# The up product of the first feed-forward block, done in seven block products for each pair of tiles

## The chip, the cores and the metric

One core of one Trainium2 chip runs the whole computation in one launch. The metric is the device time of that launch in microseconds, from the first to the last instruction and what lies around them. TensorE (PE) multiplies, VectorE (DVE), ScalarE (ACT) and GpSimd (POOL) do the rest, and SyncE (SP) issues most DMAs.

## The reference

Two transformer blocks on 1024 tokens of width 1024, all in float32. The first block is a token mixer (pooling and sparse attention) and a feed-forward block; the second is a mixer of neighbourhood attention and gated linear attention, and a feed-forward block with squared ReLU. Only the first block's feed-forward part matters here:

```python
def conv_ffn(h, w_up, conv_w, conv_b, w_down):      # D_FF = 2752, so w_up is 1024 x 5504
    u = h @ w_up
    up = jnp.pad(u, ((0, 0), (CONV_WIDTH - 1, 0), (0, 0)))
    c = conv_b + conv_w[0] * up[:, 0:S]
    for tap in range(1, CONV_WIDTH):                 # CONV_WIDTH = 3, along the tokens
        c = c + conv_w[tap] * up[:, tap:tap + S]
    gate, val = jnp.split(c, 2, axis=-1)
    return (jax.nn.silu(gate) * val) @ w_down
x = x + token_mixer(rms_norm(x, attn_norm_w), ...)
x = x + conv_ffn(rms_norm(x, ffn_norm_w), w_up, conv_w, conv_b, w_down)
```

## The kernel before

Activations lie transposed in SBUF: 128 features on the partitions, 1024 tokens along the row, eight such rows (`X`) for the width of 1024. Every large product is made of units: one unit is 128 output features for all 1024 tokens, from eight weight blocks of 128 by 128. To keep float32's accuracy each factor is split into a rounded part and a remainder (`WHI`, `WLO` for weights, `X_HI`, `HLO` for activations) and three products are added: hi by hi, hi by lo, lo by hi. So a full unit is 8 blocks x 3 products x 2 halves of 512 tokens = 48 matmuls of 128x128 by 512 columns (L248). ScalarE makes `WHI` (L215), VectorE makes `WLO` (L220), SyncE loads the raw weights two units ahead. `job_done` counts finished units, `evacuated` those whose accumulator (`PAIR`, two of them) has been read.

**The first feed-forward block** has 22 tiles of hidden features, 21 of them with a gate unit and a value unit, and one tail of 64 features whose gate and value rows share one unit: 43 up units. For each tile VectorE takes the accumulator times the norm's factor (`dve_scaled`, L371) into `UP`, ScalarE makes the affine part of the convolution (L1352), VectorE adds the two other taps (L1382, L1385), ScalarE applies SiLU (L1355), VectorE multiplies gate and value (L1390), and the product is split into `HID_HI` (L1372) and `HID_LO` (L1412), which stay in SBUF. After each eight tiles come eight down units that add into `X` (L1469), and after the last six tiles eight units of six blocks (36 matmuls). The two first units of the up product, and the two first of the last down group, are interleaved block by block (`pe_first_units`, L272). These stages are loops on every engine.

**The second feed-forward block** (from `U_WOUT`) already has its up product in another form, `pe_seven`, L2645. There weights and activations are cut into 2 by 2 blocks: a pair of units (1024 by 256 weights) by all tokens is one 2x2 block product, and it is formed from seven products of blocks instead of eight (Winograd's form; `FACTORS`). Each of the seven is 4 blocks x 3 products = 12 matmuls of 512 columns. What it needs around it:

- sums of the activations' blocks, `XSR`, split into `XSH` and `XSL`, made once while the units before it run (`pool_xs`, `dve_xs`, `act_xs_hi`, `dve_xs_lo`);
- for each pair four sums of weight blocks on GpSimd (`pool_ws`, L2274 to L2285), each waiting until the sum before in that buffer has been split;
- for each product a split of its 128x512 weight factor, three products ahead (`act_pw_hi` L2346, `dve_pw_lo` L2350);
- for each pair three copies of partial results out of PSUM on ScalarE (`act_part`, L2358), each of which TensorE waits for before a later product adds into the same bank (product 2 waits for copy 0, product 3 for copy 1, product 4 for copy 2), and on VectorE the sums that give the four output blocks (`dve_sum12` L2365, `dve_sum22` L2371, `dve_sum11` L2375 and L2379, `dve_sum21` L2384 and L2386). Product 6 waits for `dve_sum22`.

The order on each engine is written out by hand, product by product ("slot" j of pair q): first the sums or copies that product j-1 allows, then the split for product j+3. The finished rows go to DRAM (`hidden`) and come back through `HRAW` for the down units; the first eight come back in the last pair's slots (`HID_FIRST`).

Of the kernel before, what the change touches and what calls it, by code (L numbers as in the profile page):

```python
# [14 lines left out]
F32 = mybir.dt.float32  # L15
# [4 lines left out]
P = 128  # L20
T = 1024
# [76 lines left out]
def build(nc, a, out):  # L98
# [157 lines left out]
    def pe_first_units(pe, u, n):  # L256
# [48 lines left out]
    def pe_unit(pe, u, hi, lo, ready=None, outs=1, early=None):  # L305

        pe.wait_ge(w_lo, u + 1)
        for o in range(outs):
# [54 lines left out]
    def dve_weighted_lo(dve, n, k, x_k):  # L363
        dve.wait_ge(hhi_done, 8 * n + k + 1)
# [955 lines left out]
    def at_unit(u, more=0):  # L1320


        assert u >= U_G1
        return u % 2, 16 * (u // 2 + 1) + 8 * more, jobs_before(u) + more

    def act_split_at(act, u, more):
        slot, loaded, jobs = at_unit(u, more)
        if u < UNITS:
            split_hi(act, slot, loaded, jobs - 1)

    def dve_split_at(dve, u, more):
        if u < UNITS:
            split_lo(dve, u % 2, u + 1 + more)

    def pe_unit_at(pe, u, more, hi, lo, kcs=KC, ready=None):
        j = jobs_before(u)
        pe.wait_ge(w_lo, u + 1 + more)
        pe.wait_ge(evacuated, j - 1 + more)
        product(pe, u % 2, j % 2, hi, lo, kcs, 0, ready)

    def tap_of(q, b):
        return CONV[:, bass.ds(2 * q + b, 1), :].rearrange("p o c -> p (o c)")

    def act_ff1_conv(act, u, more, q):

        for b in range(2):
            act_split_at(act, u + b + 2, more)
            act.wait_ge(evacuated, jobs_before(u + b) + 1 + more)
            if b == 0:
                act.wait_ge(gv_done, q + 1)  # L1350
            tap = tap_of(q, b)
            nc.scalar.activation((CG, CV)[b][:, :], UP[:, :], ACT.Identity,  # L1352
                                 scale=tap[:, 2:3], bias=tap[:, 3:4]).then_inc(aff_done, 1)
        act.wait_ge(conv_done, 2 * q + 1)
        nc.scalar.activation(CG[:, :], CG[:, :], ACT.Silu).then_inc(silu_done, 1)  # L1355

    def act_ff1_tail(act, q):

        act_split(act, U_FF1_TAIL + 2)
        act.wait_ge(evacuated, jobs_before(U_FF1_TAIL) + 1)  # L1360
        act.wait_ge(gv_done, q + 1)
        tap = CONV[:, 2 * q, :]
        act.wait_ge(hm_ready, 2)
        nc.scalar.activation(CG[:, :], UP[:, :], ACT.Identity, scale=tap[:, 2:3], bias=tap[:, 3:4]).then_inc(aff_done, 1)
        act.wait_ge(conv_done, 2 * q + 1)
        nc.scalar.copy(CV[0:64, :], CG[64:P, :])
        nc.scalar.activation(CG[0:64, :], CG[0:64, :], ACT.Silu).then_inc(silu_done, 1)

    def act_ff1_store(act, q, p):

        act.wait_ge(gv_done, q + 2)
        nc.scalar.copy(HID_HI[:, bass.ds(p, 1), :], GV[:, :].unsqueeze(1)).then_inc(hid_hi, 1)  # L1372

    def dve_ff1_conv(dve, u, more, q):
        for b in range(2):
            dve_split_at(dve, u + b + 2, more)
            c, tap = (CG, CV)[b], tap_of(q, b)
            if b or u > U_FF1:
                dve.wait_ge(conv_done, 2 * q + b)
            dve_scaled(dve, 1, jobs_before(u + b), UP, more)  # L1380
            dve.wait_ge(aff_done, 2 * q + b + 1)
            nc.vector.scalar_tensor_tensor(c[:, 1:T], UP[:, 0:T - 1], tap[:, 1:2], c[:, 1:T],  # L1382
                                           ALU.mult, ALU.add).then_inc(tap_done, 1)
            dve.wait_ge(tap_done, 2 * q + b + 1)
            nc.vector.scalar_tensor_tensor(c[:, 2:T], UP[:, 0:T - 2], tap[:, 0:1], c[:, 2:T],  # L1385
                                           ALU.mult, ALU.add).then_inc(conv_done, 1)
        dve.wait_ge(silu_done, q + 1)
        dve.wait_ge(conv_done, 2 * q + 2)
        dve.wait_ge(hid_lo, q + 1)
        nc.vector.tensor_tensor(GV[:, :], CG[:, :], CV[:, :], ALU.mult).then_inc(gv_done, 1)  # L1390

    def dve_ff1_tail(dve, q):

        dve_split(dve, U_FF1_TAIL + 2)
        tap = CONV[:, 2 * q, :]
        dve.wait_ge(hm_ready, 2)
        dve.wait_ge(conv_done, 2 * q)
        dve_scaled(dve, 1, jobs_before(U_FF1_TAIL), UP)
        dve.wait_ge(aff_done, 2 * q + 1)
        nc.vector.scalar_tensor_tensor(CG[:, 1:T], UP[:, 0:T - 1], tap[:, 1:2], CG[:, 1:T],  # L1400
                                       ALU.mult, ALU.add).then_inc(tap_done, 1)
        dve.wait_ge(tap_done, 2 * q + 1)
# [7 lines left out]
    def dve_ff1_store(dve, q, p):  # L1410
        dve.wait_ge(hid_hi, q + 1)
        nc.vector.tensor_tensor(HID_LO[:, bass.ds(p, 1), :], GV[:, :].unsqueeze(1),  # L1412
                                HID_HI[:, bass.ds(p, 1), :].bitcast(F32), ALU.subtract).then_inc(hid_lo, 1)

    def pe_ff1(pe):
        hi, lo = (lambda k: HID_HI[:, k, :]), (lambda k: HID_LO[:, k, :])
        pe_first_units(pe, U_FF1, 1)
        with pe.Fori(0, FF1_FULL) as g:
            with pe.Fori(0, GROUP) as p:
                for b in range(2):  # L1420
                    pe_unit_at(pe, U_FF1 + 2 + b, 24 * g + 2 * p, hi_of(1), h_lo)
            with pe.Fori(0, KC // 2) as t:
                pe.wait_ge(hid_lo, GROUP * g + GROUP + 1)
                for b in range(2):
                    pe_unit_at(pe, U_FF1 + 2 + 2 * GROUP + b, 24 * g + 2 * t, hi, lo)
        with pe.Fori(0, FF1_REST - 2) as p:
            for b in range(2):
                pe_unit_at(pe, U_FF1_REST + b, 2 * p, hi_of(1), h_lo)
        pe_unit_at(pe, U_FF1_TAIL, 0, hi_of(1), h_lo)
        tile_ready = lambda k: pe.wait_ge(hid_lo, GROUP * FF1_FULL + k + 2)  # L1430
        for part in range(2):
            for b in range(2):
                u = U_Z2 - KC + b
                j = jobs_before(u)
                if not part:
                    pe.wait_ge(w_lo, u + 1)
                    pe.wait_ge(evacuated, j - 1)
                product(pe, u % 2, j % 2, hi, lo, FF1_REST - 1 + part, 0, None if b else tile_ready,
                        part * (FF1_REST - 1), part == 1)
        with pe.Fori(1, KC // 2) as t:  # L1440
# [1597 lines left out]
```

## Time and profile before

| | us |
|---|---|
| median of 3 runs | 3111.73 |
| lowest, highest | 3110.82, 3114.38 |
| the profiled execution's own time | 3114.16 |
| its span, first to last instruction | 3112.1 |
| TensorE busy in it | 3030.7 |
| VectorE busy | 1580.9 |
| ScalarE busy | 1266.6 |
| GpSimd busy | 489.9 |

The profile is of one execution. Its own time is 2.1 us more than its span, and 2.4 us above the median of the runs. Matmuls are pipelined: a matmul's row lasts longer than the step to the next one, so the step between starts is what counts, not the length. A few records of matmuls are missing from the trace.

### The profile page before, as it was taken

To read this page: it belongs to the slowest core of one execution; us is meant where nothing else is said; L and a number is where in the kernel's file an instruction comes from. 1 tells how busy PE (TensorE), PEld (TensorE's weight loads), DVE (VectorE), ACT (ScalarE), POOL (GpSimd) and SP (SyncE) were. 2 spreads that over 40 slices of the span, in tenths; PEclk is the share of its full clock that TensorE was granted. 3 is DMA by queue.
4 is the path that set the end of the run, shared out by engine and by line. 5 is a ranking of instruction groups with operands and counts; after the bars stand their busy time and mean duration, and the time that the engine had idled before them with its cause. 6 is when DMAs were issued, how large, how long until landed. Compare 5 with 4: busy or idle time off the path is not lost.

```text
span 3112.1 us, 42590 instructions
## 1 busy us (share of the span) xinstructions
PE 3030.7 (97%) x16760; PEld 2490.6 (80%) x16760; DVE 1580.9 (51%) x2426; ACT 1266.6 (41%) x1999; POOL 489.9 (16%) x688
## 2 busy tenths in 40 slices
PE   8999998899999999999999999999999999999998
PEld 6888887789988878888888888656878788878887
DVE  6653257667763445534542552465654755543334
ACT  4652137877773233212221341365643543431122
POOL 0110007755542000000000000120012322200000
PEclk9999998999999999999999999999999999999999
DMA  4222320000004311111111131100102233242322
GB/s 144 82 75 75 114 88 15 2 2 2 1 2 151 99 42 54 47 47 47 47 47 52 49 123 58 34 1 21 41 28 75 102 110 117 99 162 95 95 75 75
DMA packets 61189, 201.96 MB, mean 65 GB/s; under 512 B 9840, under 2 KB 13040, under 8 KB 60640
## 3 DMA queue, kind: packets, MB, share of 16 engines
q1 hardware_dynamic: 50048, 159.52, 15.6%
q0 software_dynamic: 10976, 40.15, 3.6%
q8 instruction: 114, 1.87, 0.3%
q14 instruction: 51, 0.42, 0.0%
HBM read 160.32 MB, written 33.55 MB: 62 GB/s over the span
## 4 chain that ended last, share of the span: by engine, by line
PE 91%; ACT 4%; DVE 3%; issue 2%; DMA 0%; POOL 0%; SPq 0%; DVEq 0%; ACTq 0%; POOLq 0%
PE PS L248 60%; PE PS L2645 9%; PE PS L902 3%; PE PS L916 3%; PE PS L888 2%; PE PS L887 2%; PE PS L1692 2%; PE PS L272 1%; PE PS L1719 1%; PE PS L1704 1%; ACT P_SHORT L986 1%; PE PS L939 1%; PE PS L2671 1%; ACT PT L996 1%; PE PS L930 1%
## 5 line engine op out<-in xcount | busy, mean ns | idle before, releaser
L215 ACT CAST WHI<-RAW 128x1024 fp32r<-128x1024 f32 x185 | 194.5, 1052 | 1118.7 <-PE PS L248 1094.7
L220 DVE TENSOR_TENSOR WLO<-RAW,WHI 128x1024 fp32r<-128x1024 f32 x185 | 226.7, 1225 | 606.3 <-ACT WHI L215 604.0
L248 PE MATMUL PS<-HLO,WHI 128*128 128x512 f32 x1648 | 508.1, 390 | 0.0
L248 PEld LDWEIGHTS PS<-HLO,WHI 128*128 128x128 f32 x1648 | 309.7, 188 | 64.9
L248 PE MATMUL PS<-X_HI,WHI 128*128 128x512 f32 x1008 | 312.9, 392 | 2.2 <-DVE W L371 2.2
L248 PE MATMUL PS<-X_HI,WLO 128*128 128x512 f32 x1008 | 310.9, 390 | 0.0
L248 PE MATMUL PS<-HID_HI,WHI 128*128 128x512 f32 x832 | 256.3, 389 | 2.5 <-DVE W L2375 1.3
L248 PE MATMUL PS<-HID_LO,WHI 128*128 128x512 f32 x832 | 256.2, 389 | 0.0
L248 PE MATMUL PS<-HID_HI,WLO 128*128 128x512 f32 x832 | 256.2, 389 | 0.0
L248 PEld LDWEIGHTS PS<-X_HI,WHI 128*128 128x128 f32 x1008 | 188.5, 188 | 44.5 <-DVE W L371 2.7
L248 PEld LDWEIGHTS PS<-X_HI,WLO 128*128 128x128 f32 x1008 | 189.5, 188 | 39.6
L248 PEld LDWEIGHTS PS<-HID_HI,WHI 128*128 128x128 f32 x832 | 156.0, 188 | 35.6 <-DVE W L2375 1.7
L248 PEld LDWEIGHTS PS<-HID_HI,WLO 128*128 128x128 f32 x832 | 156.2, 188 | 32.5
L248 PEld LDWEIGHTS PS<-HID_LO,WHI 128*128 128x128 f32 x832 | 156.2, 188 | 32.4
L248 PE MATMUL PS<-HHI,WHI 128*128 128x512 f32 x512 | 160.1, 394 | 2.7 <-DVE WLO L220 2.7
L248 PE MATMUL PS<-HHI,WLO 128*128 128x512 f32 x512 | 157.6, 389 | 0.0
L1469 DVE TENSOR_TENSOR XB<-XB,PS 128x1024 f32<-128x1024 f32 x30 | 36.6, 1221 | 217.4 <-PE PS L248 217.4
L887 PE MATMUL PS<-KHD,QS 128*128 128x512 f32 (+3 forms) x384 | 136.7, 363 | 4.9 <-DVE HMIN L1075 2.6
L1097 POOL TENSOR_SCALAR P_LONG<-P_LONG,HINV,GATE 128x640 f32<-128x640 f32 (+3 forms) x128 | 121.0, 956 | 93.7 <-DVE HINV L1080 93.3
L986 ACT ACTIVATE P_LONG<-P_LONG,HMIN 128x640 f32<-128x640 f32 (+3 forms) x128 | 116.7, 914 | 38.2 <-DVE HMIN L1075 37.5
L1528 POOL DMA_DIRECT2D x_kept<-X x8 | 4.2, 534 | 793.9 <-DVE X L1307 793.9
L996 ACT COPY PT<-PS 128x512 f32<-128x512 f32 x216 | 116.6, 590 | 20.9 <-PE PS L902 19.4
(401 smaller groups left out, 5910.6 us busy)
## 6 DMA issues: line engine op xcount, KB each, us to landing
RAW<-in_w SPq DMA_DIRECT2D x187, 512.0 KB, 3.5
W<-in_w SPq DMA_DIRECT2D x16, 1024.0 KB, 4.9
hidden<-W SPq DMA_DIRECT2D x32, 512.0 KB, 2.6
W<-hidden SPq DMA_DIRECT2D x32, 512.0 KB, 4.6
X<-in_x SPq DMA_DIRECT2D x8, 512.0 KB, 7.9
Q<-QN POOLq DMA_DIRECT2D x32, 128.0 KB, 2.7
merged<-W POOLq DMA_DIRECT2D x8, 512.0 KB, 3.3
W<-gate POOLq DMA_DIRECT2D x8, 512.0 KB, 4.0
```

Source lines behind the costliest of these rows:

```text
L215: nc.scalar.copy(WHI[:, slot, :], RAW[:, slot, :]).then_inc(w_hi, 1)
L220: nc.vector.tensor_tensor(WLO[:, slot, :], RAW[:, slot, :], WHI[:, slot, :].bitcast(F32), ALU.subtract).then_inc(w_lo, 1)
L248: last = nc.tensor.matmul(o[:, half], w[:, slot, cols], x(k)[:, half], start=(k == 0 and w is WHI and x is hi), stop=(done and k == kcs - ...
L887: nc.tensor.matmul(out, QS[s % 2][:, j, :], KHD[g][:, branch, c:end], start=True, stop=False)
L888: last = nc.tensor.matmul(out, QS[s % 2][:, j, :], KLD[g][:, branch, c:end], start=False, stop=True)
L902: last = nc.tensor.transpose(turn_ps(c)[:, P * (2 * x + e):P * (2 * x + e) + P], src, IDENT[:, :])
L916: last = nc.tensor.matmul(out_ps(m)[half_of(e), :], (VS, VW)[branch][:, kt, g], PT[u % 8][:, 2 * x + e, :], start=False, stop=(u + 1 == us ...
L986: nc.scalar.activation(p, p, ACT.Exp, scale=-1.0, bias=HMIN[:, n % 8, branch:branch + 1], accum_out=HSUM[:, n % 8, branch:branch + 1]).the ...
L996: nc.scalar.copy(PT[u % 8][:, 0:n, :], turn_ps(c)[:, 0:P * n].rearrange("p (x q) -> p x q", q=P))\
L1097: nc.gpsimd.tensor_scalar(p, p, HINV[:, n % 8, branch:branch + 1], GATE[:, qt, col:col + 1], ALU.mult, ALU.mult).then_inc(p_done, 1)
L1692: nc.tensor.matmul(NS_PS[n % 4], QST[n % 4][:, :], KA[:, hp, 64 * start:64 * start + 512], start=True, stop=True).then_inc(ns_done, 1)
L2645: last = nc.tensor.matmul(out2, wt[n % 4][:, cols], xt[x][:, k, :], start=(i in (0, 1, 5) and k == 0 and xt is XSH and wt is PWH), stop=(k ...
```

## The change

The first feed-forward block's up product takes the form that the second block's has. `Seven` is a class that holds what both uses need (`S1`, `S2`), and the functions get it as an argument. In `S1` an item is one tile: its gate unit and its value unit are the pair. There are 21 pairs of seven products, and the tail of 64 + 64 rows is an item of four products of its own (`TAIL_FACTORS`), put last but one. All products come first; every tile's gated rows go to DRAM (`hidden1`), and the down product follows in three groups of 8, 8 and 6 tiles, its tiles read back. The eight units before (`U_WO`) take over the making of the activations' sums. The loops of the stage are gone. The weights' order in DRAM follows. The second block's code is the same work with other names.

```diff
+    class Seven:
...
+    S1 = Seven("1", None, 1, X, U_WO, U_FF1, ["pair"] * (FF1_TILES - 2) + ["tail", "pair"],
...
+    HID1_FIRST = {1: (0,), 2: (1,), 4: (2,), 5: (3, 4), 6: (5,)}
...
+    TAIL_FACTORS = (("A11", "B11", "z"), ("A11", "T1", "w"), ("A12", "B22", "w"), ("A12", "B21", "z"))
...
+    def act_ff1_slot(act, q, i):
...
+        if i == 0:
+            act_affine(act, q, 1)
+        if i == 1:
+            act_silu(act, q)
+
+    def dve_ff1_slot(dve, q, i):
...
+        elif i == 0:
+            dve_tap1(dve, q, 0)
+            dve_tap0(dve, q, 0)
+        elif i == 1:
+            dve_tap1(dve, q, 1)
+        elif i == 2:
+            dve_tap0(dve, q, 1)
+        if i == 3:
+            dve_gated(dve, q)
...
+    def act_seven1(act):
+        for j, (q, i) in enumerate(S1.products):
+            act_seven_slot(act, S1, j)
+            act_ff1_slot(act, q - 1, i)
+            if i == 6:
+                act_affine(act, q, 0)
+            if q == Q_LAST1:
+                for h in HID1_FIRST.get(i, ()):
+                    act_hid1_hi(act, h)
+                if i == 5:
+                    act_first_down(act, S1, 0)
...
+    def dve_seven1(dve):
+        for j, (q, i) in enumerate(S1.products):
+            dve_seven_slot(dve, S1, j)
+            dve_ff1_slot(dve, q - 1, i)
+            if q == Q_LAST1:
+                for h in HID1_FIRST.get(i, ()):
+                    dve_hid1_lo(dve, h)
+                if i == 5:
+                    dve_split(dve, U_FF1)
+
+    def dve_ff1_down(dve):
+        dve_sum21(dve, S1, Q_LAST1)
+        dve_ff1_slot(dve, Q_LAST1, 0)
+        for h in (6, 7):
+            dve_hid1_lo(dve, h)
+        dve_split(dve, U_FF1 + 1)
+        for i in range(1, 4):
+            dve_ff1_slot(dve, Q_LAST1, i)
+        for d in range((FF1_GROUPS - 1) * KC):
+            dve_add_residual(dve, U_FF1 + d, 0, X, d % KC)
+            dve_split(dve, U_FF1 + d + 2)
+            if GROUP + d < FF1_TILES:
+                dve_hid1_lo(dve, GROUP + d)
+        dve_residual(dve, U_Z2 - KC, 2, X, lambda t: X[:, t, :], lambda t: None)
...
+    def sp_hidden1(sp, h):
+
+        g, k = divmod(h, GROUP)
+        q = TILE_OF.index(h)
+        sp.wait_ge(hid_out[0], 16 * (q + 1))
+        if h >= 4:
+            sp.wait_ge(hid_lo, h - 3)
+        if g == 0:
+            if k == 4:
+                sp.wait_ge(up_done, S1.up0[Q_LAST1] + 1)
+            elif k == 5:
+                sp.wait_ge(pw_lo, S1.prods)
+            else:
+                sp.wait_ge(prod_done, S1.done(Q_LAST1, (0, 0, 3, 3, None, None, 5, 5)[k]))
+        elif g == 1:
+            sp.wait_ge(prod_done, S1.prods)
+        else:
+            sp.wait_ge(job_done, jobs_before(U_FF1 + KC * (g - 1)))
+        sp.dma_start(HID1_RAW[g % 2][k][:, :], hidden1[h]).then_inc(HID1_IN[h % 4], 16)
...
+        for h in range(GROUP):
+            if h == 2:
+                store(Q_LAST1 - 1)
+            sp_hidden1(sp, h)
...
+    def pe_ff1_down(pe):
+        for d in range(FF1_GROUPS * KC):
+            g = d // KC
+            if d < 2:
+                pe.wait_ge(up_done, S1.up0[Q_LAST1] + (3, 5)[d])
+            ready = None if d % KC else lambda k: pe.wait_ge(hid_lo, GROUP * g + k + 1)
+            pe_unit(pe, U_FF1 + d, lambda k: HID1_HI[g % 2][k][:, :], lambda k: HID1_LO[g % 2][k][:, :], ready=ready,
+                    kcs=FF1_REST if g == FF1_GROUPS - 1 else KC)
...
     def pool_second(pool):
 
-        pool.wait_ge(merged_done, KC)
+        pool.wait_ge(prod_done, S1.prods)
...
-        pe_ff1(pe)
+        pe_seven(pe, S1)
+        pe_ff1_down(pe)
```

`act_affine` is the affine part of the convolution (gate b=0, value b=1), `dve_tap1` and `dve_tap0` the two taps, `act_silu` and `dve_gated` as before, each of tile q-1 in the slots of item q. `dve_sum11` and `dve_sum21` multiply by the norm's factor where the second block also takes the ReLU.

## Rows read from the trace of the kernel before

**Rows 1.** The page: busy time, share of span and instructions of TensorE.

```profile
PE 3030.7 (97%) x16760; PEld 2490.6 (80%) x16760; DVE 1580.9 (51%) x2426; ACT 1266.6 (41%) x1999; POOL 489.9 (16%) x688
```

**Rows 2.** Chain of waits, 1040 to 1900: start us, length us, what.

```profile
1135.03 10.89 PE PS L272 x48
...
1159.57 1.15 DVE W L371
...
1160.76 637.00 PE PS L248 x2802
...
1799.01 1.15 DVE WLO L220
...
1849.53 10.89 PE PS L272 x48
```

**Rows 3.** TensorE's timeline in the first up product: first and last of 49 rows.

```profile
1299.83 0.62 PE L248 MATMUL PS<-X_HI,WHI 128*128 128x512 f32 x2
...
1321.59 0.62 PE L248 MATMUL PS<-X_HI,WHI 128*128 128x512 f32 x2
```

**Rows 4.** Chain of waits, 2330 to the end.

```profile
2432.04 5.44 PE PS L2645 x24
2437.48 4.53 issue
2442.01 8.38 PE PS L2645 x24
2450.39 1.72 PE PS L325 x4
2452.11 277.46 PE PS L2645 x1224
...
2749.13 326.69 PE PS L248 x1440
```

**Rows 5.** VectorE by line and form, 2460 to 2740 (seven products): count | busy us, mean ns.

```profile
L2350 DVE TENSOR_TENSOR PWL<-WS_S,PWH 128x512 fp32r<-128x512 f32 x59 | 40.5, 687 | 23.5 <-ACT PWH L2346 23.2
...
L2379 DVE SCALAR_TENSOR_TENSOR W<-W,W 128x1024 f32<-128x1024 f32 x15 | 18.9, 1261 | 0.5
L2386 DVE SCALAR_TENSOR_TENSOR W<-W,W 128x512 f32<-128x512 f32 x15 | 17.0, 1131 | 0.0
...
L2375 DVE TENSOR_TENSOR W<-PART,PS 128x512 f32<-128x512 f32 x14 | 9.6, 688 | 18.5 <-PE PS L2645 18.5
```

**Rows 6.** VectorE by line and form, 1140 to 1790 (first feed-forward block).

```profile
L1382 DVE SCALAR_TENSOR_TENSOR W<-W,CONV,W 128x1023 f32<-128x1023 f32 x42 | 53.9, 1284 | 72.2 <-ACT W L1352 72.2
...
L1390 DVE TENSOR_TENSOR W<-W,W 128x1024 f32<-128x1024 f32 x21 | 25.7, 1225 | 1.9
```

**Rows 7.** ScalarE by line and form, 2460 to 2740.

```profile
L2346 ACT CAST PWH<-WS_S 128x512 fp32r<-128x512 f32 x58 | 35.8, 617 | 58.8 <-PE PS L2645 58.8
...
L2358 ACT COPY PART<-PS 128x512 f32<-128x512 f32 x45 | 26.1, 581 | 44.8 <-PE PS L2645 44.8
```

**Rows 8.** ScalarE by line and form, 1140 to 1790.

```profile
L1352 ACT ACTIVATE W<-W,CONV 128x1024 f32<-128x1024 f32 x42 | 52.2, 1244 | 115.7 <-DVE W L371 115.7
L1355 ACT ACTIVATE W<-W 128x1024 f32<-128x1024 f32 x21 | 21.9, 1045 | 0.0
```

**Rows 9.** GpSimd's timeline: start us, length us, what, idle before.

```profile
2422.69 1.74 POOL L2278 TENSOR_TENSOR WS_S<-WS_S,W 128x512 f32<-128x512 f32 x1
...
2555.42 1.29 POOL L2278 TENSOR_TENSOR WS_S<-WS_S,W 128x512 f32<-128x512 f32 x1 [2.52 <-DVE PWL L2350]
```

**Rows 10.** VectorE's timeline at the same times.

```profile
2423.31 1.67 DVE L2260 SCALAR_TENSOR_TENSOR XSR_T<-XB,NORM_W,XSR_T 128x512 f32<-128x512 f32 x1
...
2556.12 1.14 DVE L2386 SCALAR_TENSOR_TENSOR W<-W,W 128x512 f32<-128x512 f32 x1
```

**Rows 11.** ScalarE's timeline, last pair of the second block's up product.

```profile
2736.26 1.05 ACT L2407 CAST HID_HI<-W 128x1024 fp32r<-128x1024 f32 x1 [2.67 <-DMA W<-hidden]
```

**Rows 12.** The page: DMA issues, KB each, median us from issue to landing.

```profile
W<-hidden SPq DMA_DIRECT2D x32, 512.0 KB, 4.6
```

More of the change, by code:

```diff
@@ L1344, in act_ff1_conv @@
[L1344 to L1355, printed above, removed]
@@ L1369, in act_ff1_store @@
[L1369 to L1390, printed above, removed]
@@ L1410, in dve_ff1_store @@
[L1410 to L1440, printed above, removed]
-            for b in range(2):
-                pe_unit_at(pe, U_Z2 - KC + b, 2 * t, hi, lo, FF1_REST)
@@ L2288, in pool_seven, with pool_seven1, pool_seven2 @@
+    def pool_seven1(pool):
+        for t in range(4):
+            pool_xs(pool, S1, t)
+        for q, kind in enumerate(S1.items):
+            if kind == "pair":
+                pool_ws(pool, S1, q)
+    def pool_seven2(pool):
         pool.wait_ge(gl_lo, GLA_HEADS)
@@ new lines, in act_part, with dve_sum12, dve_sum22 @@
+        nc.scalar.copy(c.part[i][:, :], c.banks[q % 2]["zwz"[i]]).then_inc(part_done, 1)
+    def dve_sum12(dve, c, q):
+        dve.wait_ge(prod_done, c.done(q, 3))
+        dve.wait_ge(part_done, c.part0[q] + 3)
+        if c is S2 and q:
+            dve.wait_ge(hid_out[0], 16 * (FF1_TILES + q))
+        nc.vector.tensor_tensor(c.up[0][:, HI_COLS], c.part[2][:, :], c.banks[q % 2]["w"], ALU.add).then_inc(up_done, 1)
+    def dve_sum22(dve, c, q):
+        dve.wait_ge(prod_done, c.done(q, 4))
+        if c is S2 and q:
+            dve.wait_ge(hid_out[1], 16 * q)
+        nc.vector.tensor_tensor(c.up[1][:, HI_COLS], c.part[1][:, :], c.banks[q % 2]["z"], ALU.add).then_inc(up_done, 1)
@@ new lines, in build, with convs_before, act_affine @@
+    Q_TAIL = S1.items.index("tail")
+    def convs_before(q, b=0):
+        return 2 * q + b - (1 if q > Q_TAIL else 0)
+    def act_affine(act, q, b):
+        n_up = 4 if b == 0 and q != Q_TAIL else 6 if b else 3
+        act.wait_ge(up_done, S1.up0[q] + n_up)
+        if b:
+            if q:
+                act.wait_ge(hid_out[0], 16 * q)
+        elif q:
+            act.wait_ge(gv_done, q)
+        if q == Q_TAIL:
+            act.wait_ge(hm_ready, 2)
+        tap = CONV[:, 2 * TILE_OF[q] + b, :]
+        nc.scalar.activation((CG, CV)[b][:, :], S1.up[b][:, :], ACT.Identity,
+                             scale=tap[:, 2:3], bias=tap[:, 3:4]).then_inc(aff_done, 1)
@@ new lines, in act_seven_slot @@
+    def act_seven_slot(act, c, j):
+        q, i = c.products[j]
+        if i in (1, 2, 3) if c.items[q] == "pair" else i == 1:
+            act_part(act, c, q, i - 1)
+        if j + 3 < len(c.products):
+            act_pw_hi(act, c, j + 3)
+        if q == 0 and i < 4:
+            for m, k in XS_AFTER[i]:
+                act_xs_hi(act, c, m, k)
+        if j == 4:
+            act_rstd(act, c.norm)
+    def act_seven1(act):
[3 more added lines that the diff above has]
+            if i == 6:
+                act_affine(act, q, 0)
+            if q == Q_LAST1:
[3 more added lines that the diff above has]
+                    act_first_down(act, S1, 0)
@@ L2557, in dve_wout, with dve_seven_slot @@
                 for m, k in XS_TURN:
-                    dve_xs_lo(dve, m, k)
-    def dve_seven(dve):
-        for j in range(PRODS + 1):
-            q, i = divmod(j, NP)
+                    dve_xs_lo(dve, c, m, k)
+    def dve_seven_slot(dve, c, j):
+        q, i = c.products[j]
+        if c.items[q] == "pair":
             if i == 4:
-                dve_sum12(dve, q)
+                dve_sum12(dve, c, q)
             if i == 5:
-                dve_sum22(dve, q)
+                dve_sum22(dve, c, q)
@@ new lines, in dve_seven_slot @@
+        if i == 0 and q:
+            if c.items[q - 1] == "pair":
+                dve_sum21(dve, c, q - 1)
+            else:
+                dve_tail_lo(dve, q - 1)
+        if j + 3 < len(c.products):
+            dve_pw_lo(dve, c, j + 3)
+        if j == 0:
+            dve_acc(dve, c.norm, KC - 1)
+        if q == 0 and i < 4:
+            for m, k in XS_AFTER[i]:
+                dve_xs_lo(dve, c, m, k)
+    def dve_seven1(dve):
[7 more added lines that the diff above has]
+                    dve_split(dve, U_FF1)
@@ L2580, in dve_seven, with dve_seven2 @@
+    def dve_seven2(dve):
+        for j, (q, i) in enumerate(S2.products):
+            dve_seven_slot(dve, S2, j)
+            if q == Q_LAST2:
+                for h in HID_FIRST.get(i, ()):
                     dve_hid_lo(dve, h)
@@ L2582, in dve_seven @@
                     dve_split(dve, U_FF2)
+        dve_sum21(dve, S2, Q_LAST2)
     def dve_ff2_down(dve):
```

744 lines of the change are left out of this document (393 added, 351 removed).

## The prediction

> **What bounds the kernel now.** I read the page first: TensorE is busy for 97% of the span [rows 1]. A busy share alone can hide a slow step, so next I read how far apart its matmuls start. In the first block's up product 49 rows of two matmuls go from 1299.83 to 1321.59 [rows 3]: 21.76 us / 96 = 0.2267 us for each. Then the chain of waits over the stage [rows 2]: from the first up matmul (1135.03) to the first of the next stage (1849.53) are 714.5 us, nearly all of it TensorE. Counted from the code the stage has 43 x 48 up and 16 x 48 + 8 x 36 down = 3120 matmuls: 707.2 us, and 1.7 for the norm's mean; 5.5 us are left, in gaps behind the interleaved units (the chain leaves TensorE at 1159.57 and 1799.01). So the stage costs what its matmuls cost, and only fewer matmuls, or new gaps, can move it.
>
> The second block shows what the new form does on this chip. From 2452.11 the chain is TensorE alone, 277.46 us for 1224 matmuls [rows 4], 0.2267 each: same step, no gap, in spite of a new weight factor for each matmul. Only its ends cost something.
>
> **What goes.** 21 gate units and 21 value units are 21 x 96 = 2016 matmuls; as pairs they are 21 x 84 = 1764. The tail is 48 either way, the down product 1056 either way. 252 matmuls go: 252 x 0.2267 = 57.1 us. The 5.5 us of old gaps go with the code that made them. So 62.6 us at most, if nothing new stands on TensorE's path.
>
> **What comes at the start.** The units before must now also make the sums of X. In the second block that work came late for product 2: 24 matmuls in 5.44 us, then nothing for 4.53, then 24 in 8.38 [rows 4]. The missing 2.94 us are matmuls whose starts lie wider apart just after the idle time. The order on every engine is copied, and X is ready as early there, so I take the same 4.53 + 2.94 = 7.5 us. Bounds: 4.5 (no slow matmuls) to 10.
>
> **What comes in each pair.** TensorE takes 84 x 0.2267 = 19.04 us for one, a product 2.72. All else must fit beside it. VectorE, from [rows 5, 6]: seven splits 7 x 0.69, the four sums that read PSUM 4 x 0.69, the value tile's second half times the norm 0.69, the gate tile times the norm 1.22 (the length of L1390's form), four taps 4 x 1.28, gate by value 1.22: 15.8 us. ScalarE [rows 7, 8]: seven splits 7 x 0.62, three copies 3 x 0.58, two affine parts 2 x 1.24, SiLU 1.05: 9.6 us. Both fit, VectorE with 3.2 us to spare.
>
> But GpSimd's four sums of weights, 1.29 us each [rows 9], disturb VectorE. The one that starts at 2555.42 ends at 2556.71, and the VectorE multiplication that starts at 2556.12 in between, both of its inputs in SBUF, lasts 1.14 instead of 0.69 [rows 9, 10]: it ends 0.55 after GpSimd does. At 2423.31 a three-operand form takes 1.67, while GpSimd's own sum beside it takes 1.74 [rows 9, 10]: they take turns. The taps and the product of gate and value read two inputs from SBUF too, and here they stand in slots 0 to 3, just where the second block left VectorE idle for GpSimd. Worst case: all four sums block, 15.8 + 4 x 1.29 = 21.0 us, 2.0 over. I laid the pair out by these lengths, zero being TensorE's start of product 0, and with engines seeing a product's end some 0.2 later. VectorE: two halves of dve_sum21 to 2.0 (one blocked for 0.5), split to 2.6, first gate tap to 3.8, GpSimd's third sum to 5.0, second gate tap to 6.1, split, first value tap to 7.9, GpSimd's fourth sum to 9.0, split, second value tap to 10.8, split, gate by value to 12.5, dve_sum12 to 13.1 (2 late), split, and at 13.8 dve_sum22 is on time again. GpSimd's first sum falls into an idle stretch. So about two and a half sums block, and the pair closes with TensorE never waiting for a sum: product 6 starts at 16.3, dve_sum22 is done at 14.5. The narrow place is on ScalarE: SiLU is queued ahead of the copy of partial 1. It waits for the second gate tap (6.1), runs to 7.1, the copy to 7.7, and TensorE wants product 3 at 8.16. 0.45 us to spare. I count nothing per pair, with bounds 0 and 2.0.
>
> The Trainium skill, page "SBUF — State Buffer", section "Who interferes with whom", says that VectorE and GpSimd share one port pair as an exclusive lock: a VectorE instruction with two SBUF inputs and a GpSimd instruction that reads SBUF block each other for the whole length of the one that came first. That speaks against this change, which puts five long instructions of that kind beside GpSimd in each pair. The trace agrees with its 1.14 and 1.67 us for half tiles. By the rule at its worst the pair is the 21.0 us of rival 2; by the layout it costs nothing, since GpSimd is held up as well and its sums are not urgent.
>
> **What comes at the end.** The first eight hidden tiles must be back from DRAM and split before the down product. The last pair's slots get eight splits of 1.22 us on VectorE and eight of 1.05 on ScalarE, in order, so they stand before copies and sums that TensorE wants. In the second block two tiles were fetched long before, and yet ScalarE waited 2.67 us for one DMA [rows 11]; from 2432.04 to the down product at 2749.13 are 317.1 us [rows 4], less 1344 x 0.2267 = 304.7, the mean's 1.7 and the start's 7.5, so that end cost 3.2 us. Here it is worse in two places. (a) Tile 0 is fetched only after product 0 of the last pair (2.7), lands 4.6 later at the median [rows 12] and is split to 8.5, before partial 1 is copied: product 3 starts 0.8 late. Behind it stand the tail's copy and SiLU and tile 1's split, so partial 2 comes at 13: product 4 is 1.2 late. (b) SP issues the fetch of tile 2 behind the tail tile's store, which waits for VectorE's gate by value: VectorE comes 3 late out of the tail (taps of tile 19 packed in four products, and four sums of GpSimd in a row), so that is at about 16. Tile 2 lands about 20.5, is split on both engines to 22.7, and dve_sum22 stands behind it, at 23.4: product 6, due at 18.4, starts 5.0 late and its twelve matmuls are wide apart, 2.6 to 2.9 more. The last splits then hold up the first down unit by some 0.4. Sum: 0.8 + 1.2 + 5.0 + 2.8 + 0.4 = 10.2 us. Bounds 3.2 (as in the second block) and 14 (twice the DMA's wait).
>
> Nothing is added later. The groups' other tiles have a down unit of 10.9 us each for one fetch, one 1.05 and one 1.22 split; the constants that pool_second loads are wanted hundreds of microseconds on.
>
> **Sum.** 2868 x 0.2267 + 1.7 + 7.5 + 10.2 = 669.6 us instead of 714.5: 44.9 less. Against the profiled execution, 3114.2 - 44.9 = 3069.3; that one lies 2.4 above the median, so the median should be 3111.7 - 44.9 = 3067.
>
> **Rivals.**
> 1. *A cheap end.* Tiles land in 3 us and the tail's VectorE lag is small: the end costs the second block's 3.2 instead of 10.2, so 3060. For it: the copy of its order. Against: tile 2's place behind the store.
> 2. *VectorE becomes the bound.* All four GpSimd sums block in every pair: 21 x 2.0 = 41 us back, 3108. For it: the port's price is in [rows 10]. Against: the first sum meets an idle or PSUM-reading VectorE.
> 3. *Product 3 waits a little in each pair.* If the second gate tap is 0.9 later than I laid it out, TensorE waits 0.45 x 20 = 9 us: 3076.
> 4. *Slower.* The same place, partial 1's copy behind SiLU, with GpSimd getting its turn before both gate taps and the split between them: two more blocks of up to 1.74 [rows 9] put the tap at 9.6, SiLU to 10.7, the copy to 11.3, 3.1 late in each of 20 pairs: 62 us, 3129. It decides from 2.2 us a pair (44.9 / 20). Against: GpSimd has only four sums, and two of them are due in slots 5 and 6.
>
> **Numbers.** Chances: the forecast 0.60 (its own range 3062 to 3073), rival 1 0.12, rival 3 0.18, rival 2 0.05, rival 4 0.05. The range runs from rival 1's side to past rival 3's: 3056 to 3084, leaving out rivals 2 and 4 and a bit of each tail. A measurement of this kernel tells about 0.2% (6 us) from no change. Faster 0.91, the same 0.03 (rival 2 in part), slower 0.06 (rival 4, and what I overlook of it).
>
> **What would show it.** From the first seven-product matmul to the next stage's first interleaved unit 670 us. The chain there is TensorE at 0.2267 a matmul from product 4 of pair 0 to the last pair. One gap of some 4.5 before product 2 of pair 0, and gaps before products 3, 4 and 6 of the last pair, the last of them released by dve_sum22. VectorE's taps last 1.28 or about 2.3 by turns. The prediction is wrong if TensorE's waits name the partial copies in every pair, or if the chain runs through VectorE's taps.

## The result, and the profile after

The changed kernel takes 3086.7 us (median of 4 runs, 3083.5 to 3091.1), the kernel before, beside it on the same chip, 3113.1. The ratio is 0.9916, with an interval of 0.9899 to 0.9934: 26.4 us faster, where 45 were forecast, and 2.7 us outside the range.

The page of the execution profiled (its own time is 3091.09 us), with the chain's shares by engine:

```profile
span 3089.3 us, 41962 instructions
...
PE 2993.6 (97%) x16508; PEld 2455.4 (79%) x16508; DVE 1743.7 (56%) x2650; ACT 1345.9 (44%) x2191; POOL 666.6 (22%) x780
...
PE 83%; DVE 9%; ACT 4%; issue 3%; DMA 1%; POOL 0%; SPq 0%; ACTq 0%; DVEq 0%; POOLq 0%
```

TensorE is still busy for 97% of the span. The share tells nothing of the loss; the chain does, which now runs through VectorE for 9%. Its pieces in the stage (start, length, what), which answer to [rows 2] and [rows 4]:

```profile
1139.65 5.44 PE PS L2786 x24
1145.09 4.58 issue
1149.67 8.15 PE PS L2786 x24
...
1294.29 8.46 PE PS L2786 x36
...
1303.49 1.22 DVE W L2273
...
1310.17 2.21 DVE W L2331
...
1314.08 8.46 PE PS L2786 x36
...
1511.98 27.50 PE PS L2786 x120
...
1557.42 6.25 DMA HID_RAW<-hidden
...
1573.53 5.13 DMA HID_RAW<-hidden
...
1595.22 231.49 PE PS L256 x1020
1826.71 10.89 PE PS L280 x48
```

The first unit of the next stage begins at 1826.71, so the stage takes 687.1 us; it took 714.5 [rows 2], and 669.6 were predicted. The group from 1294.29 to 1314.08 is one pair, and it repeats: from 1195.34 to 1511.98 are 316.64 us for 16 pairs, 19.79 each, where 84 matmuls take 19.04. So the account of the stage is

| us | predicted | measured |
|---|---|---|
| 2868 matmuls at 0.2267, and the mean | 651.9 | 651.9 |
| start (issue 4.58, and 8.15 where 24 matmuls take 5.44) | 7.5 | 7.3 |
| pairs (16 x 0.75, and 0.4 in the first one that waits) | 0 | 12.4 |
| end | 10.2 | 15.2 |
| stage | 669.6 | 686.8 |

The end is 1595.22 less 1511.98, 83.2 us, less the 22 products (59.84) up to the down product and the 36 matmuls (8.16) ahead of 1595.22. The 0.3 us that the sum lacks of 687.1 are what my counting of gaps leaves over.

The stage is 27.4 us shorter, the span only 22.8. The other 4.6 lie ahead of the change: this stage begins at 1139.65 instead of 1135.03 [rows 2]. Most of it arises in a stretch of the attention stage, which the change doesn't touch (busy time of each engine; the number after POOL's is the granted clock of TensorE), in the kernel after:

```profile
400.00:600.00 200.00, 186.75 (x1318) 160.64 (x1318) 126.76 (x416) 131.04 (x333) 95.03 (x140) 0.91 0.10 35
```

and in the kernel before:

```profile
400.00:600.00 200.00, 180.82 (x1339) 154.91 (x1338) 128.51 (x427) 134.67 (x342) 98.49 (x144) 0.96 0.10 35
```

Laid side by side, ScalarE's instructions of the two traces are 0.5 us apart at 423 us of the kernel before, 3.7 at 575 and 4.6 at 676. The clock granted there differs between executions; that it accounts for all of the 3.2 us is a reading, not a test. In the executions of the experiments the span less the stage is 2395 to 2402 us, whatever was edited: a single time can't tell 5 us, a stage's length in the trace can. It is not free of chance either: the wait at the start, 4.6 us here, is 5.5 in e1 and 3.7 in e2, and e1's edit doesn't touch it.

**Where a pair's 0.75 us go.** Instructions by time (start, length, and in brackets the idle time before it with its releaser) in the stretch that ends with a pair's product 3 at 1314.08:

```profile
1303.49 1.22 DVE L2273 TENSOR_TENSOR W<-W,W 128x1024 f32<-128x1024 f32 x1
...
1303.77 2.10 POOL L2158 TENSOR_TENSOR WS_S<-W 128x512 f32<-128x512 f32 x1 [8.24 <-DMA W<-in_w]
...
1304.63 1.79 DVE L2243 TENSOR_TENSOR PWL<-WS_S,PWH 128x512 fp32r<-128x512 f32 x1
...
1306.50 1.29 POOL L2162 TENSOR_TENSOR WS_S<-WS_S,W 128x512 f32<-128x512 f32 x1 [0.63 <-DVE PWL L2243]
...
1306.94 1.40 DVE L2283 TENSOR_TENSOR W<-W,W 128x512 f32<-128x512 f32 x1
...
1309.02 2.27 POOL L2166 TENSOR_TENSOR WS_S<-W,WS_S 128x512 f32<-128x512 f32 x1 [1.23 <-DVE PWL L2243]
...
1310.17 2.20 DVE L2331 SCALAR_TENSOR_TENSOR W<-W,CONV,W 128x1022 f32<-128x1022 f32 x1
...
1312.40 1.06 ACT L2341 ACTIVATE W<-W 128x1024 f32<-128x1024 f32 x1 [1.80 <-DVE W L2331]
1313.37 0.57 ACT L2251 COPY PART<-PS 128x512 f32<-128x512 f32 x1
...
1314.08 0.47 PE L2786 MATMUL PS<-XSH_B,PWH 128*128 128x512 f32 x1 [0.47 <-ACT PART L2251]
```

Read it from the bottom. Product 3 waits for the copy of partial 1 (L2251, 1313.37). The copy stands behind SiLU (L2341), which had to wait for the second gate tap (L2331), done at 1312.37. Between VectorE's instructions GpSimd's sums get their turns: the split at 1304.63 lasts 1.79 instead of 0.69, the half multiplication 1.40, the tap 2.20 instead of 1.28. TensorE started the pair at 1305.29: product 3 was due at 1313.45, one step behind the matmul before it (1313.22), and three products go off that. I had laid out `dve_sum21` done 2.0 after it; it is done at 1308.34, 3.05 after. The tap is 7.1 after it instead of 6.1, the copy 8.65 instead of 7.7, and 8.16 was the limit.

The first of the sums is the one out of place. It should have run while VectorE was idle, and was released by a DMA. SyncE's issues in the kernel after:

```profile
1297.91 0.37 SPq L2550 DMA_DIRECT2D W<-in_w  x1
1299.04 0.34 SPq L2555 DMA_DIRECT2D hidden<-W  x1
```

and in the second block of the kernel before, where a pair starts at 2555.31, with GpSimd's first sum:

```profile
2546.49 0.38 SPq L2486 DMA_DIRECT2D W<-in_w  x1
...
2551.61 1.29 POOL L2274 TENSOR_TENSOR WS_S<-W 128x512 f32<-128x512 f32 x1 [9.22 <-DVE PWL L2350]
...
2555.86 0.32 SPq L2491 DMA_DIRECT2D hidden<-W  x1
```

There the pair's 1 MB of weights are asked for 8.8 us ahead of the pair's start, and are no longer waited for 3.7 ahead of it, when a split releases the sum. Here they are asked for 7.4 ahead, since VectorE's last splits of the pair before come later, a store follows 1.1 us behind, and they are there 5.9 us after their issue, 1.5 ahead of the start at 1305.29. So they are issued 1.4 us later, and take longer too: 4.7 to 5.1 us for the eleven loads of the second block, 5.6 to 6.0 for the sixteen from 1198.96 to 1495.80. The stage's loads at 1139.7 and 1159.4, behind which no store is issued so soon, took 4.8 us here too. That points at the store; no run moved it. The second block is near the same edge: in its next pair, at 2570.65, the DMA is what releases the first sum. Ahead of the pair that starts at 1305.29 VectorE is idle from 1301.4 to 1302.8; its weights, there at 1303.77, miss that by a microsecond.

**Where the end's 15.2 us go.** SyncE's queue, and the two gaps of TensorE:

```profile
1555.76 0.33 SPq L2555 DMA_DIRECT2D hidden<-W  x1
1556.13 1.20 SPq L2572 DMA_DIRECT2D RAW<-in_w  x2
1557.42 0.91 SPq L2413 DMA_DIRECT2D HID_RAW<-hidden  x2
...
1565.37 0.77 PE L2786 MATMUL PS<-XSH_B,PWH 128*128 128x512 f32 x1 [4.13 <-ACT PART L2251]
...
1573.11 0.32 SPq L2555 DMA_DIRECT2D hidden<-W  x1
1573.53 2.16 SPq L2413 DMA_DIRECT2D HID_RAW<-hidden  x4
...
1581.72 0.77 PE L2786 MATMUL PS<-XSH_T,PWH 128*128 128x512 f32 x1 [5.15 <-DVE W L2264]
```

Tile 0 is fetched at 1557.42, behind a store and two loads of the down weights, and lands at 1563.69. ScalarE takes its split first and the copy of partial 1 after it, so TensorE stands idle for 4.13 us. After that its matmuls are 0.427 us apart until 1571.4; the granted clock says what that is:

```profile
1565.40:1570.60 5.20, 5.20 (x12) 4.11 (x13) 2.95 (x4) 4.38 (x6) 0.00 (x0) 0.50 0.00 0
```

0.50 is the lower level, 1.2 GHz. In gaps between starts, less one step, and in what the wide steps cost, place (a) makes 4.29 + 2.86 = 7.15 us, and place (b), at 1581.72, 5.31 + 1.61 = 6.92. One more microsecond goes before 1595.22, to the last tiles' splits.

### The profile page after: what moved, and what is told of

Read it like the earlier page. It is cut to its first block, busy times and chain, and to the rows that moved or that the text cites. A ratio compares the mean times of both kernels' runs of the same rounds, so it can differ in the third digit from the quotient of the medians.

```text
span 3089.3 us, 41962 instructions
## 1 busy us (share of the span) xinstructions
PE 2993.6 (97%) x16508; PEld 2455.4 (79%) x16508; DVE 1743.7 (56%) x2650; ACT 1345.9 (44%) x2191; POOL 666.6 (22%) x780
## 4 chain that ended last, share of the span: by engine, by line
PE 83%; DVE 9%; ACT 4%; issue 3%; DMA 1%; POOL 0%; SPq 0%; ACTq 0%; DVEq 0%; POOLq 0%
PE PS L256 46%; PE PS L2786 16%; PE PS L912 3%; PE PS L926 3%; PE PS L898 2%; PE PS L897 2%; PE PS L1531 2%; DVE PWL L2243 1%; DVE W L2331 1%; PE PS L1558 1%; PE PS L1543 1%; PE PS L949 1%; ACT P_SHORT L996 1%; DVE W L2273 1%; DVE W L2283 1%
## 5 line engine op out<-in xcount | busy, mean ns | idle before, releaser
L256 PE MATMUL PS<-HLO,WHI 128*128 128x512 f32 x992 | 306.5, 390 | 0.0
L256 PE MATMUL PS<-HID_HI,WHI 128*128 128x512 f32 x832 | 256.5, 389 | 2.4 <-DVE W L2268 1.6
L256 PE MATMUL PS<-HID_LO,WHI 128*128 128x512 f32 x832 | 256.2, 389 | 0.0
L256 PE MATMUL PS<-HID_HI,WLO 128*128 128x512 f32 x832 | 256.0, 389 | 0.0
L2786 PE MATMUL PS<-XSH_T,PWH 128*128 128x512 f32 x596 | 236.2, 396 | 15.5 <-issue 9.1
L2786 PE MATMUL PS<-XSL_T,PWH 128*128 128x512 f32 x596 | 234.5, 393 | 0.0
L2786 PE MATMUL PS<-XSH_T,PWL 128*128 128x512 f32 x596 | 234.2, 393 | 0.0
L256 PEld LDWEIGHTS PS<-HLO,WHI 128*128 128x128 f32 x992 | 186.7, 188 | 39.3
L2786 PE MATMUL PS<-XSH_B,PWH 128*128 128x512 f32 x456 | 180.1, 395 | 12.1 <-ACT PART L2251 12.1
L256 PEld LDWEIGHTS PS<-HID_HI,WHI 128*128 128x128 f32 x832 | 156.0, 188 | 35.5 <-DVE W L2268 2.0
L256 PEld LDWEIGHTS PS<-HID_LO,WHI 128*128 128x128 f32 x832 | 156.2, 188 | 32.6
L256 PEld LDWEIGHTS PS<-HID_HI,WLO 128*128 128x128 f32 x832 | 156.2, 188 | 32.3
L2786 PE MATMUL PS<-XSH_B,PWL 128*128 128x512 f32 x456 | 178.7, 392 | 0.0
L2786 PE MATMUL PS<-XSL_B,PWH 128*128 128x512 f32 x456 | 178.5, 391 | 0.0
L256 PE MATMUL PS<-HHI,WHI 128*128 128x512 f32 x512 | 160.7, 395 | 2.7 <-DVE WLO L228 2.7
L256 PE MATMUL PS<-HHI,WLO 128*128 128x512 f32 x512 | 158.1, 390 | 0.0
L2239 ACT CAST PWH<-WS_S 128x512 fp32r<-128x512 f32 x148 | 90.9, 616 | 138.7 <-PE PS L2786 138.7
L2786 PEld LDWEIGHTS PS<-XSH_T,PWH 128*128 128x128 f32 x596 | 113.4, 190 | 42.0 <-issue 17.9
```

What stands on the lines that cost most here:

```text
L256: last = nc.tensor.matmul(o[:, half], w[:, slot, cols], x(k)[:, half], start=(k == 0 and w is WHI and x is hi), stop=(done and k == kcs - ...
L2239: nc.scalar.copy(c.pwh[n % 4][:, :], c.raw_of(n)).then_inc(pw_hi, 1)
L2786: last = nc.tensor.matmul(c.banks[q % 2][b], wt[n % 4][:, cols], xt[x][:, k, :], start=(opens and k == 0 and xt is c.xsh and wt is c.pwh), ...
```

## The experiments

Before each, the theory it tests was written down. The ratios are to the kernel before, run beside each on the same chip. *A* below is the reading above: the copy behind SiLU in each pair, and the fetched tiles' splits ahead of copies and sums at the end.

| | edit | us (runs) | ratio and interval | stage |
|---|---|---|---|---|
| after | | 3086.7 (4) | 0.9916, 0.9899 to 0.9934 | 687.1 |
| e1 | SiLU one slot later | 3077.5 (4) | 0.9889, 0.9872 to 0.9905 | 675.2 |
| e2 | GpSimd's sums 64 columns | 3071.9 (1) | | 671.8 |
| e3 | value tile's weights first | 3072.4 (1) | | 672.8 |
| e4 | tiles read back later | 3080.0 (4) | 0.9901, 0.9885 to 0.9918 | 678.6 |
| e5 | e1 and e4 | 3068.3 (5) | 0.9850, 0.9837 to 0.9864 | 667.2 |
| e6 | e1, e3 and e4 | 3066.9 (1) | | 664.5 |
| e7 | e5, other order of X sums | 3070.0 (4) | 0.9858, 0.9843 to 0.9873 | 667.1 |
| e8 | after, other order of X sums | 3085.4 (1) | | 687.2 |
| e9 | e6's kernel once more | 3065.5 (5) | 0.9849, 0.9836 to 0.9862 | 664.5 |
| e10 | e9, last taps behind splits | 3067.4 (5) | 0.9850, 0.9837 to 0.9862 | 664.3 |

### e1: SiLU one slot later

```diff
-        if i == 1:
+        if i == 2:
             act_silu(act, q)
...
-        act_ff1_slot(act, Q_LAST1, 1)
+        act_ff1_slot(act, Q_LAST1, 2)
...
```

> SiLU goes from slot 1 to slot 2 on ScalarE, behind the copy of partial 1; nothing else moves. Theory A: in each pair TensorE waits 0.75 us because that copy is queued behind SiLU, and nothing else is short; so the step from pair to pair falls from 19.79 to 19.04 us, the waits for the partial copies in pairs 2 to 18 go, and the stage (first seven-product matmul to the next stage's first unit) falls from 687.1 to about 674.6. Theory B: VectorE is the bound (18.1 us busy of 19.79, and it is blocked by GpSimd); then TensorE's wait moves to another signal of VectorE and the step stays at 19.5 or more, the stage at 684 or more.

Measured: stage 675.2, 11.9 less. The chain of waits has one piece of TensorE from the first pair to the one ahead of the tail:

```profile
1158.52 367.22 PE PS L2786 x1620
```

1620 x 0.2267 is 367.2, so all 12.4 us of the pairs' waits are gone; the start is 0.6 dearer in this execution. SiLU still waits for the second gate tap, and the copy of partial 1 has gone ahead of it:

```profile
1305.44 0.59 ACT L2251 COPY PART<-PS 128x512 f32<-128x512 f32 x1 [0.32 <-PE PS L2786]
...
1306.91 1.06 ACT L2341 ACTIVATE W<-W 128x1024 f32<-128x1024 f32 x1 [0.37 <-DVE W L2331]
```

VectorE's instructions have kept their lengths, splits of 1.78 and taps of 2.20. So it isn't VectorE's load that holds TensorE up but one instruction's place in ScalarE's order.

### e2: sums of 64 columns

```diff
-        s1, s2, s4, s3 = (c.ws[m][:, :] for m in ("S1", "S2", "S4", "S3"))
+        n = 64 if c is S1 and q else 512
+        s1, s2, s4, s3 = (c.ws[m][:, 0:n] for m in ("S1", "S2", "S4", "S3"))
...
```

> GpSimd's four sums of weights cover 64 of their 512 columns from the second pair on (the other columns keep old values, so the products are of other numbers), same count and same signals. Theory A: what makes SiLU late is GpSimd's sums blocking VectorE; with sums of some 0.3 us all VectorE instructions have their plain lengths (taps 1.28, splits 0.69), the second gate tap ends 1.5 us or more earlier, the step is 19.04 us and the stage about 674.6, with SiLU where it was. Theory B2: the port has little to do with it, the gate tap is late because of VectorE's own queue; then the step stays within 0.2 of 19.79.

Measured: stage 671.8. The waits of the pairs are gone here too, with SiLU at its old place: taps last 1.28, splits 0.69. GpSimd's blocks are what made the tap late. The stage is 2.8 us shorter than expected, which I hadn't counted: 2.3 at the end, where TensorE's wait for the copy in the last pair is 2.6 instead of 4.1 us and fewer matmuls are wide apart, and 0.6 at the start.

### e3: the value tile's weights first

The pair's weights come in two DMAs of 512 KB with a semaphore each; the first sum needs the value tile's alone.

```diff
-                sp.dma_start(S1.w7[q % 2][:, :, :], a["w"][at_q:at_q + 2].rearrange("h p n -> p h n"))\
-                    .then_inc(pair_in[q % 2], 16)
+                sp.dma_start(S1.w7[q % 2][:, 1, :], a["w"][at_q + 1]).then_inc(second_in[q % 2], 16)
+                sp.dma_start(S1.w7[q % 2][:, 0, :], a["w"][at_q]).then_inc(pair_in[q % 2], 16)
...
```

> The weights of a pair come in two DMAs of 512 KB instead of one of 1 MB, the value tile's first, and GpSimd's first sum, which needs only that, waits for it alone. Theory A: the step that failed is where the first sum falls. It now starts some 2 us earlier, in the stretch in which VectorE waits for product 5, so the gate multiplication (1.22) and the split after it (0.69) are not blocked, dve_sum21 is done 1.0 us earlier, and the step is 19.04 us, the stage about 675. Rival: the four sums cost VectorE the same wherever they fall, and the step stays at 19.6 or more.

Measured: stage 672.8. The same stretch by time:

```profile
1313.33 1.29 POOL L2159 TENSOR_TENSOR WS_S<-W 128x512 f32<-128x512 f32 x1 [6.39 <-DVE PWL L2247]
...
1315.22 1.22 DVE L2277 TENSOR_TENSOR W<-W,W 128x1024 f32<-128x1024 f32 x1
1316.37 0.68 DVE L2247 TENSOR_TENSOR PWL<-WS_S,PWH 128x512 fp32r<-128x512 f32 x1
```

The first sum waits for a split, no longer for the DMA, and is over before the gate multiplication starts: 1.29 us, the split behind it 0.68. The second gate tap still lasts 2.20, and yet TensorE doesn't wait. One block too many was the whole difference. Of the 2 us under the expected stage, the end again has the most (waits of 2.9 and 5.9 us, with fewer matmuls wide apart). Three different edits (e1 to e3) each remove all of the wait.

### e4: the tiles read back later

```diff
-    HID1_FIRST = {1: (0,), 2: (1,), 4: (2,), 5: (3, 4), 6: (5,)}
+    HID1_FIRST = {3: (0,), 4: (1,), 6: (2, 3, 4, 5)}
...
-            if h == 2:
+            if h == 4:
                 store(Q_LAST1 - 1)
```

> Only the last item changes: the first hidden tiles are split in slots 3, 4 and 6 (one, one, four tiles) instead of slots 1, 2, 4, 5, 6, and SyncE issues the fetches of tiles 2 and 3 before the tail tile's store. Theory A: the end costs 15.2 us because splits that wait for DMAs stand ahead of the copy of partial 1 (4.1 us) and of dve_sum22 (5.2 us plus slow matmuls); both waits go, the down product starts within 2 us of its due time, and of 15.2 us some 4 stay (stage about 676), with a wait of 1 to 2 us for the splits of tiles 6 and 7. Rival: the DMAs themselves are late (6 us each behind one another), so the wait moves to the down unit's own blocks and no more than 5 us are won (stage 682 or more).

Measured: stage 678.6, 8.5 less; about 676 had been expected. TensorE's waits in the stage (total, times, longest):

```profile
PE PS L2786 <- ACT PART L2251: 8.7, 18, 0.6
...
PE PS L256 <- DVE HID_LO L2423: 3.2, 2, 2.5
PE PS L2786 <- DVE W L2264: 1.4, 1, 1.4
```

The waits of 4.1 and 5.2 us have fallen to 0.6 and 1.4, and the pairs' stay. What I had underrated is the wait of the down unit (L256): four tiles are now split at the very end, and the first down unit waits 0.7 us for the first of them and 2.5 for tile 6.

### e5: both

> SiLU in slot 2 and the new order at the end together. Theory A: the two losses are apart (pairs 2 to 18, and the last item), so the gains add: stage 687.1 - 11.9 - 8.5 = 666.7 us, and the whole kernel about 20 us under the changed kernel. Rival: with SiLU later, the tail's gate by value and store come later too and eat part of the end's gain; then 669 or more.

Measured: stage 667.2, against 687.1 - 11.9 - 8.5 = 666.7. The gains add up to within 0.5 us: the two losses are independent.

### e6 and e9: all three

> The same with the pair's weights in two DMAs, the value tile's first. Theory A: in the pairs either edit alone already takes the wait away, so both together give nothing more there; only VectorE's lag out of the tail can be smaller. Stage within 1.5 us of the run without it. Rival: the port's blocks cost something besides product 3; then 3 us or more less.

> The run with SiLU in slot 2, two weight DMAs and the new end once more, timed. In the profile before its stage was 664.5 us, 22.6 under the changed kernel's 687.1, and no edit touches another stage. Theory A: 3086.7 less 22.6 is about 3064 us. Rival: the 2.7 us that its stage was under the run without the two DMAs are chance (a stretch of wide-apart matmuls in the down product); then its stage comes out at 667 here.

Measured: stage 664.5 in both, 2.7 us less than e5, more than the 1.5 expected of e6. The chain of e9:

```profile
1156.67 388.98 PE PS L2791 x1716
...
1569.72 231.52 PE PS L256 x1020
```

It runs on TensorE alone for 389 us, into the last pair. From 1156.67 to the last piece's start are 413.05 us, in e5 414.10: 1.05 us come from the end, where e5 still waits 0.6 us for a copy. The other 1.6 are matmuls of e5's down product around 1571 to 1574, whose starts lie wide apart behind the wait for the last tiles (granted clock 0.79 from 1568 to 1576); e9 waits 2.5 us at the same place too and has no such stretch. Nor has e4, which waits there as long and has its weights in one DMA, so the stretch doesn't hang on that edit alone; whether the edit has a part in it is open. In time the two kernels can't be told apart: their intervals are nearly the same.

### e7 and e8: another order of the X sums

```diff
-    XS_TURN = [("B11", k) for k in range(4)] + [("B22", k) for k in range(3)] + T_OF(2)
+    XS_TURN = [("B11", k) for k in range(4)] + [("T2", 2)]
...
```

The rest of B22 and T3 is made after the last rows of X, behind T2's.

> SiLU and end as before, and a new order of the splits of the activations' sums at the start, in both blocks: before TensorE's product 0 only those that products 0 to 2 need (5 instead of 10 on VectorE), the rest behind. Theory A for the start: the gap of 4.6 us before product 2 comes from VectorE, which adds the last unit to X 5 us late behind ten splits, so ScalarE's copy of partial 0 is late; with five fewer splits (3.3 us) the gap falls to about 1.3 us and the matmuls behind it are wide apart for less long. Each block wins 3 to 6 us; stage about 662. Rival: the gap is set by GpSimd's sums beside dve_xs (blocked to 1.65 us each), and stays above 3.5 us.

> The new order at the start alone, on the changed kernel. Theory A: 3 to 6 us less in each block's first pair, the rest of the stage as it was (step 19.79 us, end 15 us): stage 681 to 684. Rival as in the run with all three: the gap stays above 3.5 us, stage 686 or more.

Measured: stages 667.1 and 687.2, nothing won: both miss. In e7 the wait before product 2 has fallen from 4.6 to 0.5 us, and come back behind it:

```profile
1141.09 0.47 PE L2787 MATMUL PS<-XSH_T,PWH 128*128 128x512 f32 x1 [0.50 <-issue]
...
1144.01 0.50 PE L2787 MATMUL PS<-XSH_T,PWH 128*128 128x512 f32 x1 [0.64 <-DVE XSL_T L2221]
...
1147.47 0.77 PE L2787 MATMUL PS<-XSH_B,PWH 128*128 128x512 f32 x1 [2.48 <-DVE XSL_B L2225]
```

Behind the last one the granted clock is 0.50 again. The second block, which has the new order too, wins 0.9 us at its start in e7 (18.8 us from its first matmul to product 4, against 19.7 in e5), not 3. The theory that the order of the X sums costs the start its time has fallen. VectorE is at work without a break from the last rows of X until product 3, and what is moved ahead of one product comes late for the next. That reading is from the traces alone; no run made that work smaller.

### e10: the last taps behind the last splits

```diff
-        dve_ff1_slot(dve, Q_LAST1, 0)
         for h in (6, 7):
             dve_hid1_lo(dve, h)
         dve_split(dve, U_FF1 + 1)
+        dve_ff1_slot(dve, Q_LAST1, 0)
```

> The same, and at the turn to the down product VectorE splits tiles 6 and 7 and the second weights before the last gate tile's two taps, not behind them. Theory A: TensorE waited 0.7 and 2.5 us for splits of hidden tiles in the first down unit, the second time behind 2.6 us of taps; that wait falls to 1 us or less, the stage by about 1.5 to 2.5 us. Rival: tile 7's DMA lands too late for it (ScalarE waited 0.7 us for it), and less than 1 us is won.

Measured: stage 664.3, 0.2 less. The first down unit still waits 3.0 us, 2.3 of them for tile 6. The chain ahead of it:

```profile
1559.92 4.63 DVE HID_LO L2427 x4
...
1565.79 1.24 ACT W L2323
1567.04 0.94 ACT HID_HI L2422
...
1568.00 1.24 DVE HID_LO L2427
...
1569.28 231.53 PE PS L256 x1020
```

So under 1 us is won, as the rival said, but not for its reason. ScalarE waited 0.2 us for tile 7's DMA, behind this; tile 6 was fetched at 1561.2 and landed 4.3 us later, 1.4 before ScalarE split it. What stood ahead of the split was the value tile's affine part (L2323, 1565.79), which waits for `dve_sum21` behind VectorE's four splits. Again it is an order on ScalarE; no run changed it.

## Why the prediction came out as it did

**What was right.** The step of 0.2267 us and the 252 matmuls that go: 2868 of them and the mean fill the stage but for the named losses. The start, taken from the second block's own start at 7.5 us, is 7.3. The place of every wait that came is in the text: product 3 behind the copy behind SiLU, the copies and `dve_sum22` of the last pair behind tiles 0 and 2. Rival 1 is out, the end cost 15.2. Rival 2 is out: VectorE is busy for 18.1 of 19.8 us in a pair, not the bound, as e1 shows by leaving its load alone. Rival 4 too; the tap was 1.0 late, not 3.5.

**What failed** is the term per pair, taken as 0 for "GpSimd's first sum falls into an idle stretch". It doesn't, since it waits for its weights. I had copied the second block's idle stretch without asking when the DMA in front of it is issued and what is issued beside it: 1.4 us later than there, with a store at its heels and a landing some 0.8 us longer, so that the sum starts 2.2 us later. With all four sums blocking instead of two and a half, VectorE was about 1 us late, and the margin was 0.45. TensorE's waits name the partial copies in the pairs from 2 to 18, the sign by which the prediction called itself wrong. Rival 3 named this place with 9 us for a tap 0.9 later. It was 12.4, since TensorE's restart costs more than the copy's delay: the copy ended 0.49 behind the limit, product 3 was due at 1313.45 and came at 1314.08, 0.63 late, the step behind its first matmul is 0.30, and all in all a pair loses 0.75. e1 took these waits away.

In the new rows a sum of GpSimd behind a running multiplication of VectorE takes 2.10 us, and the split behind that sum 1.79. The Trainium skill, page "SBUF — State Buffer", section "Who interferes with whom", has it that a VectorE instruction with two SBUF inputs contends with a GpSimd instruction that reads SBUF, and that the order of issue decides which of them waits; the rows agree. The error was not in the rule but in when the sum started.

**What was mis-sized** is the end, 15.2 instead of 10.2. Place (b) was worked out at 5.0 + 2.8 and measured 5.3 + 1.6. Place (a) was put at 0.8 + 1.2 and measured 7.15: I took the fetch of tile 0 as issued at once and 4.6 us long, without the store and the two weight loads that stand ahead of it on SyncE (issued at 1555.76 to 1557.3), and it took 6.25. And I gave wide-apart matmuls to the longer wait only, though a wait of 4.1 us has them too. The last tiles were 0.4 and measured 1.0.

**The rest.** The 4.6 us ahead of the stage are of the profiled execution: the medians differ by 26.4 us, the stages of the two profiles by 27.4, so that of the two spans' 22.8 the missing part is nearly all chance.

The best version, e9, has the repairs of e1, e3 and e4: 3065.5 us. That it comes so near the 3067 forecast for a kernel without a wait in its pairs is in part luck: its end costs some 5 us where 10.2 were forecast, and its stage is 5.1 us under the 669.6. The start still costs 7.

## What to carry to other kernels

When a schedule is copied from another stage, look at when its DMAs are issued and not only at its engines' order: a buffer freed one or two microseconds later shifts the one instruction that everything was laid around. Where a layout leaves TensorE less than a microsecond, take the wait as the likely case, and look, in the queue of the engine that TensorE waits for, for the instruction that nobody wants soon (here SiLU on ScalarE, 11.9 us for one line moved). At the turn between two stages, list all that stands in a DMA queue ahead of the first fetch, and put the splits of what is fetched behind the copies that TensorE waits for.

## What the runs showed of the hardware

- After idle times of 4.1, 4.6 and 5.2 us TensorE's matmuls are 0.427 us apart instead of 0.227, at a granted clock of 0.50, and that costs 1.6 to 2.9 us more. After the 0.47 us in each pair they aren't. After 2.6 us in e2's last pair they are too, at 1.7 us more. After 2.5 us in the first down unit they were in e5 and e7, and not in e4, e6 and e9.
- GpSimd's sum of 64 columns takes 0.33 us in e2, and 1.30 when VectorE's tap of 1.28 us has just begun (at 1300.44, the sum at 1300.61): a small instruction of GpSimd pays for the rest of VectorE's.
- A load of 1 MB lands in 4.7 to 5.1 us in the second block, and in 5.6 to 6.0 in the first block's stage, where a store of 512 KB is issued 1.1 us behind it.
- The granted clock in the attention stage (400 to 600 us) is 0.91 in one execution and 0.96 in another, and the first falls 3.2 us behind the other from 423 to 575.
